# A transformer block with a mixture of experts: blocks of 32 slots on four column groups, longer runs of weights, and near buffers for half of the next expert

## The reference, cut to what matters

```python
logits = xt @ router_w + router_b                # 256 x 32
top_v, top_e = lax.top_k(logits, 4)
wts = softmax(top_v)
hgu = xb @ w_gate_up[e] + b_gate_up[e]           # 1024 -> 2048
gate, up = split(hgu, 2)
gate = minimum(gate, 7.0); up = clip(up, -7.0, 7.0)
act = (up + 1.0) * (gate * sigmoid(1.702 * gate))
y = act @ w_down[e] + b_down[e]                  # 1024 -> 1024
```

```text
2 127 71 46 36 3 24 88 50 22 16 23 33 11 17 99 61 5 28 28 7 3 9 30 27 16 15 37 2 20 16 52
```

## Time and profile before

| | us |
|---|---|
| median of 3 runs | 1495.45 |
| lowest, highest | 1490.48, 1495.61 |
| the profiled execution | 1494.09 |
| its span | 1492.1 |
| TensorE, VectorE, ScalarE, GpSimd busy | 1395.6, 450.2, 254.9, 10.6 |

### The profile page before, as it was taken

The page is one execution under the profiler, slowest core; times in us unless marked ns, Lnnn a source line. Parts: engine busy times, 40 slices in busy tenths (PEclk is TensorE's granted clock), DMA queues, the critical chain, the costliest instruction groups (busy, mean ns, idle before and its releaser), DMA issues.

```text
span 1492.1 us, 17242 instructions
## 1 busy us (share of the span) xinstructions
PE 1395.6 (94%) x6391; PEld 619.5 (42%) x6392; DVE 450.2 (30%) x965; ACT 254.9 (17%) x435; POOL 10.6 (1%) x34
## 2 busy tenths in 40 slices
PE   5999999999969999999999999999999999989996
PEld 3888455777533333333333333233333333223321
DVE  2240033131252332332333333233333332323233
ACT  3311024100021111111111111111111111111111
POOL 0000000100000000000000000000000000000000
PEclk9999999999978999999999999999999999999998
DMA  9734332788546367999699999979999999999994
GB/s 353 258 117 166 116 134 92 256 301 321 191 168 264 146 265 288 418 418 419 245 419 417 417 419 419 417 306 413 418 418 419 416 418 419 418 417 417 419 419 200
DMA packets 113087, 483.37 MB, mean 324 GB/s; under 512 B 10102, under 2 KB 10266, under 8 KB 80202
## 3 DMA queue, kind: packets, MB, share of 16 engines
q1 hardware_dynamic: 111666, 477.95, 80.2%
q0 software_dynamic: 1056, 4.06, 0.9%
q10 hardware_dynamic: 344, 1.07, 0.2%
HBM read 482.00 MB, written 1.05 MB: 324 GB/s over the span
## 4 chain that ended last, share of the span: by engine, by line
PE 72%; DMA 12%; SPq 9%; ACT 4%; issue 1%; DVE 1%; DVEq 0%; ACTq 0%
PE bank L1383 23%; PE bank L1074 14%; PE bank L1412 13%; DMA gu_slot<-in_w_gate_up 10%; PE bank L1083 7%; SPq L335 4%; SPq L340 4%; PE bank L1342 4%; PE bank L1358 3%; PE bank L1351 1%; DMA piece<-in_w_ada 1%; ACT gx L636 1%; ACT xg L638 1%; ACT actT L640 1%; PE bank L1062 1%
## 5 line engine op out<-in xcount | busy, mean ns | idle before, releaser
L1383 PE MATMUL bank<-gu_slot,xg 128*64 128x512 f32 x2304 | 518.4, 597 | 17.2 <-DMA gu_slot<-in_w_gate_up 16.5
L1383 PEld LDWEIGHTS bank<-gu_slot,xg 128*64 128x64 f32 x2304 | 159.5, 137 | 364.7 <-issue 307.5
L1412 PE MATMUL bank<-dn_slot,actT 128*64 128x512 f32 x1152 | 255.1, 595 | 24.7 <-ACT actT L640 24.7
L994 DVE TENSOR_TENSOR rowt<-bank,gt 128x512 f32<-128x512 f32 x144 | 92.8, 687 | 397.2 <-PE bank L1358 396.0
L1074 PE MATMUL bank<-hT,piece 128*128 128x256 f32 x704 | 155.5, 383 | 0.4 <-DMA piece<-in_w_in 0.4
L1412 PEld LDWEIGHTS bank<-dn_slot,actT 128*64 128x64 f32 x1152 | 79.5, 137 | 177.2 <-issue 143.9
L1074 PEld LDWEIGHTS bank<-hT,piece 128*128 128x128 f32 x704 | 134.3, 192 | 21.2 <-issue 2.0
L634 ACT ACTIVATE sig<-gcl 128x512 f32<-128x512 f32 x36 | 22.7, 630 | 569.2 <-DVE gcl L1012 569.2
L1012 DVE TENSOR_SCALAR gcl<-bank 128x512 f32<-128x512 f32 x36 | 24.9, 691 | 273.2 <-PE bank L1383 273.2
L998 DVE TENSOR_TENSOR xs<-xs,rowt 128x512 f32<-128x512 f32 x144 | 93.1, 688 | 2.5
L1083 PE MATMUL bank<-piece,hT 128*128 128x512 f32 x192 | 83.4, 593 | 0.0
(11 more groups left out here) (278 smaller groups left out, 772.6 us busy)
## 6 DMA issues: line engine op xcount, KB each, us to landing
gu_slot<-in_w_gate_up SPq DMA_DIRECT2D x256, 1024.0 KB, 17.2
dn_slot<-in_w_down SPq DMA_DIRECT2D x128, 1024.0 KB, 17.5
piece<-in_w_in SPq DMA_DIRECT2D x17, 2048.0 KB, 8.7
piece<-in_w_ada SPq DMA_DIRECT2D x12, 2048.0 KB, 15.0
piece<-in_w_branch_a SPq DMA_DIRECT2D x2, 2048.0 KB, 7.9
piece<-in_w_branch_b SPq DMA_DIRECT2D x2, 2048.0 KB, 8.6
piece<-in_w_out SPq DMA_DIRECT2D x2, 2048.0 KB, 10.5
xs<-in_x ACTq DMA_DIRECT2D x1, 1024.0 KB, 8.8
```

Of the source, the lines that this page charges most:

```text
L994: ins = V.tensor_tensor(rowt[:, t, :], sum_bank[t][q][:], gt2[:, cols_], ALU.mult)
L1383: ins = M(bank[u][64 * q:64 * q + 64, :], xg[:, k % 4, 64 * (k // 4):64 * (k // 4) + 64], gu_slot[k][:, cols_], start=(k == 0), stop=(k == ...
L1412: ins = M(bank[5][64 * q:64 * q + 64, :], actT[:, f % 4, 64 * (f // 4):64 * (f // 4) + 64], dn_slot[f // 2][:, f % 2, 512 * q:512 * q + 51 ...
```

## The change

- A block has 32 slots. Gate-up, bias, gather and down run on four column groups of 32: each group makes a quarter of the output columns (256 gate and 256 up in one product of 512, or 256 down columns). The scatter has four row groups of 32 into four PSUM banks, in two turns; the second waits for the first (`scatter_half`).
- The order of a block on TensorE is new: gate-up pieces 0 and 1, gather of the next block, down of the block before, gate-up piece 2, bias, piece 3, scatter and transposes, transposes of the hidden values.
- The sum over blocks stays in four PSUM banks; `add_rows` is gone. The expert bias rows start it, behind block 0 (`bias_done`). VectorE copies the transposed hidden values.
- Gate-up weights come in four pieces of 2 MiB with two neighbouring rows per partition, a run of 16 KB; down in four pieces of 1 MiB in runs of 8 KB.
- Pieces 0 and 1 of both, of expert e+1, are loaded into near buffers (`gu_land`, `dn_land`, 6 MiB), and GpSimd copies them into the slots when the last block of expert e has used these: eight copies of 128x1024 for gate-up and four for down, per expert. Pieces 2 and 3 are loaded straight into their slots, once they are used. Expert 1's near pieces are loaded ahead of the loop.
- Each expert has at least one block.

The core of the diff (in the TensorE part only new and kept lines):

```diff
 PAD = -2.0e38
-SLOTS = 64
+SLOTS = 32
...
         piece = [sb(f"piece{i}", 16 * i, [P, KT, 512]) for i in range(NP2)]
-        gu_slot = [sb(f"gu_slot{j}", 8 * j, [P, 2048]) for j in range(8)]
+        gu_slot = [sb(f"gu_slot{j}", 16 * j, [P, 2, 2, D]) for j in range(4)]
...
+        gu_land = [sb(f"gu_land{q}", 136 + 16 * q, [P, 2, 2, D]) for q in range(2)]
+        dn_land = [sb(f"dn_land{q}", 168 + 8 * q, [P, 2, D]) for q in range(2)]
...
-        sum_bank = [[bank[6], bank[7]], [bank[4], bank[5]]]
+        hid_bank, y_bank, turn_bank, xgT_bank = bank[4], bank[5], bank[6], bank[7]
+        sum_bank = [[bank[0], bank[1]], [bank[2], bank[3]]]
...
+            def gate_up_rows(e, q):
+                rows = slice(2 * P * q, 2 * P * (q + 1))
+                return (w_gate_up[0, e, rows, :].rearrange("(p r) n -> p (r n)", r=2) if isinstance(e, int) else
+                        w_gate_up[0, ds(e, 1), rows, :].rearrange("a (p r) n -> p (a r n)", r=2))
...
+            def load_gate_up(e, q):
+                sp.dma_start(gu_slot[q][:].rearrange("p r u n -> p (r u n)"), gate_up_rows(e, q)).then_inc(gu_in[q], 16)
...
-                user = [last for n, (_, _, last) in enumerate(PIECES) if n % NP2 == j // 2][-1]
+                    load_down(0, 2 * (kind == "wb") + i)
+            for q in range(4):
+                user = [last for n, (_, _, last) in enumerate(PIECES) if n % NP2 == q][-1]
                 wait_tile(sp, user)
-                load_expert_piece(0, j)
+                load_gate_up(0, q)
+            sp.wait_ge(bias3_ready, 1)
+            land_gate_up(1, 0)
+            wait_tile(sp, "rp")
...
+            sp.wait_ge(h2_ready, 4)
...
+            sp.wait_ge(bias_done, 1)
+            land_down(1, 1)
...
+            def second_half(e):
+                free = sp.value_load(table_used[0:1, e:e + 1] if isinstance(e, int) else table_used[0:1, ds(e, 1)],
+                                     min_val=1, max_val=MAXB + 1)
+                for q in (2, 3):
+                    sp.wait_ge(gu_in[q], 16 * e)
+                    sp.wait_ge(gu_used[q] if q < 3 else gu_full, free)
+                    load_gate_up(e, q)
+                for q in (2, 3):
+                    sp.wait_ge(dn_in[q], 16 * e)
+                    sp.wait_ge(dn_used[q] if q < 3 else y_full, free)
+                    load_down(e, q)
+            with sp.Fori(1, E - 1) as e:
+                second_half(e)
+                for q in range(2):
+                    sp.wait_ge(gu_in[q], 16 * e + 16)
+                    land_gate_up(sp.snap(e + 1), q)
+                for q in range(2):
+                    sp.wait_ge(dn_in[q], 16 * e + 16)
+                    land_down(sp.snap(e + 1), q)
+            second_half(E - 1)
...
+            pool.wait_ge(tables_ready, 1)
+            with pool.Fori(1, E) as e:
+                free = pool.value_load(table_used[0:1, ds(e, 1)], min_val=1, max_val=MAXB + 1)
+                for q in range(2):
+                    pool.wait_ge(gu_near[q], 16 * e)
+                    pool.wait_ge(gu_used[q], free)
+                    for r in range(2):
+                        for u in range(2):
+                            nc.gpsimd.tensor_copy(gu_slot[q][:, r, u, :], gu_land[q][:, r, u, :]).then_inc(gu_in[q], 4)
+                for q in range(2):
+                    pool.wait_ge(dn_near[q], 16 * e)
+                    pool.wait_ge(dn_used[q], free)
+                    for r in range(2):
+                        nc.gpsimd.tensor_copy(dn_slot[q][:, r, :], dn_land[q][:, r, :]).then_inc(dn_in[q], 8)
         @block.scalar
...
-                act.wait_ge(selwT_full, g1_)
-                A(selwT[:], bank[1][:, 0:T], ACT.Copy).then_inc(selw_out, 1)
-                act.wait_ge(y_full, g2_)
-                A(ysb[:], bank[5][:], ACT.Copy).then_inc(y_out, 1)
+                take_gathered(g2_)
+                take_rows_out(g1_)
+                gate_curve(g1_)
+                take_turned(g2_)
+                take_weights(g1_)
+            take_rows_out(act.snap(nb + 1))
             step(A(warm[:, 0:1], ident[:, 0:1], ACT.Sqrt))
...
+            def hidden(full_count, count):
+                dve.wait_ge(gu_full, full_count)
+                V.tensor_scalar(gcl[:], hid_bank[:, 0:256], LIMIT, None, ALU.min).then_inc(gcl_ready, 1)
+                V.tensor_scalar(hid_bank[:, 256:512], hid_bank[:, 256:512], LIMIT, -LIMIT, ALU.min, ALU.max)
+                dve.wait_ge(sig_ready, count)
+                V.scalar_tensor_tensor(gcl[:], hid_bank[:, 0:256], LIMIT, sig[:], ALU.min, ALU.mult).then_inc(gs_ready, 1)
+                dve.wait_ge(gs_ready, count)
+                V.scalar_tensor_tensor(act_t[:], hid_bank[:, 256:512], 1.0, gcl[:], ALU.add, ALU.mult).then_inc(act_ready, 1)
+                dve.wait_ge(actT_full, count)
+                V.tensor_copy(actT[:].rearrange("p r s -> p (r s)"), turn_bank[:, 0:256]).then_inc(actT_out, 1)
...
+                g2_ = dve.snap(g + 2)
+                e_next = dve.value_load(table_e[0:1, ds(g + 1, 1)], min_val=0, max_val=E - 1)
+                e_after = dve.value_load(table_e[0:1, ds(g + 2, 1)], min_val=0, max_val=E - 1)
+                hidden(g2_, g1_)
                 dve.wait_ge(selwT_full, g1_)
-                select_weights(e, ds(g + 1, 1))
-            dve.wait_ge(acc_out, dve.snap(nb + 1))
-            for t in range(TT):
-                dve.wait_ge(last_full, t + 1)
+                select_weights(e_next, ds(g + 1, 1))
+                dve.wait_ge(gath_full, g2_)
+                dve.wait_ge(selw_ready, g2_)
+                next_slots(g2_)
+                select(e_after)
...
+                for t in range(TT):
+                    for c in range(GROUPS):
+                        ins = M(turn_bank[32 * c:32 * c + 32, 0:256], sel[:, t, :], h2[:, t, 256 * c:256 * c + 256],
+                                start=(t == 0), stop=(t == TT - 1))
+                ins.then_inc(gath_full, 1)
+            def gather_transposes():
+                for r in range(2):
+                    ins = nc.tensor.transpose(xgT_bank[:, r * P:(r + 1) * P], gx[:].rearrange("p (i r) -> p r i", r=2)[:, r, :],
+                                              ident[:])
+                ins.then_inc(gxT_full, 1)
+            def weight_transposes():
+                for t in range(TT):
+                    ins = nc.tensor.transpose(y_bank[:, t * P:(t + 1) * P], selw[:, t, :, :].rearrange("p a s -> p (a s)"), ident[:])
+                ins.then_inc(selwT_full, 1)
+            def hidden_transposes():
+                for r in range(2):
+                    ins = nc.tensor.transpose(turn_bank[:, r * P:(r + 1) * P], act_t[:].rearrange("p (i r) -> p r i", r=2)[:, r, :],
+                                              ident[:])
+                ins.then_inc(actT_full, 1)
+            def gate_up(q, landed):
+                pe.wait_ge(gu_in[q], landed)
+                for r in range(2):
+                    for c in range(GROUPS):
+                        ins = M(hid_bank[32 * c:32 * c + 32, :], xg[:, r, 32 * q:32 * q + 32],
+                                gu_slot[q][:, r, :, 256 * c:256 * c + 256], start=(q == 0 and r == 0), stop=(q == 3 and r == 1))
+                ins.then_inc(gu_used[q] if q < 3 else gu_full, 1)
+            def gate_up_bias():
+                for c in range(GROUPS):
+                    M(hid_bank[32 * c:32 * c + 32, :], esel[:],
+                      bias3[:].rearrange("p (u n) -> p u n", u=2)[:, :, 256 * c:256 * c + 256], start=False, stop=False)
+            def down(landed):
+                for q in range(4):
+                    pe.wait_ge(dn_in[q], landed)
+                    for r in range(2):
+                        for c in range(GROUPS):
+                            ins = M(y_bank[32 * c:32 * c + 32, 0:256], actT[:, r, 32 * q:32 * q + 32],
+                                    dn_slot[q][:, r, 256 * c:256 * c + 256], start=(q == 0 and r == 0), stop=(q == 3 and r == 1))
+                    ins.then_inc(dn_used[q] if q < 3 else y_full, 1)
+            def scatter(turn, last=False):
+                for c in range(GROUPS):
+                    t = (c + turn) % 2
+                    ins = M(sum_bank[t][c // 2][:, 256 * (c % 2):256 * (c % 2) + 256], selwT[32 * c:32 * c + 32, t * P:(t + 1) * P],
+                            ysb[32 * c:32 * c + 32, :], start=False, stop=(last and turn == 1))
+                if last and turn == 1:
+                    ins.then_inc(last_full, 1)
+                if turn == 0:
+                    ins.then_inc(scatter_half, 1)
+            def bias_rows():
                 for t in range(TT):
                     for q in range(2):
+                        ins = M(sum_bank[t][q][:], wT[:, t * P:(t + 1) * P], bd[:, 512 * q:512 * q + 512], start=True, stop=False)
+                ins.then_inc(bias_done, 1)
             pe.wait_ge(bias3_ready, 1)
             pe.wait_ge(tables_ready, 1)
```

(44 more changed lines are left out.)

276 lines of the change are left out of this document (102 added, 174 removed).

## The result

| | us |
|---|---|
| median of 4 runs after | 1540.20 (1535.68 to 1545.03) |
| median of 4 runs before | 1495.43 (1490.48 to 1495.61) |
| ratio | 1.0307, 95% interval 1.0271 to 1.0343 |
| profiled execution, its span | 1535.68, 1534.0 |

A forecast was written before the change was run, and what follows sets the result against it. TensorE bound the early blocks, DMA the late experts at nearly equal price. From 475 us, 889 of loads and 77.6 of surpluses reach 1441; last blocks and end make 1486, with clock and median offset 1493; range 1470 to 1540.

The forecast's parts named there:

- Between the last gate-up and the next block lies a chain: TensorE's wait from a block's last gate-up through VectorE's and ScalarE's steps and two transposes: 3.0 us per block.
- 14.5 us. Bounds: 13.9 [...] 15.5: TensorE's time per block of 32 slots: gate-up 6.95, bias 0.22, gather 0.87, down 3.5 and chain 3.0.
- two more register loads cost 1: At the start, before block 0's gate-up: two added register loads cost 1 us, against 2.5 saved on gather and copies.
- the clock was held at full speed wherever blocks crowd: Experts with several blocks: TensorE at full clock, 14.5 us a block; half clock was expected only after rests in one-block experts.
- The pair of two-block experts 3 and 4 takes 29.0 a piece on TensorE and adds none: Two-block experts 3 and 4: TensorE's 29.0 us each stays under the 29.64 of loads, so no surplus.
- 77.6 forecast: Total surplus over 29.6 us an expert: expert 1 22.5, expert 2 14.2, expert 7 11.0, expert 15 25.5, plus restarts.
- the clock's 4 us: One-block experts: half clock after TensorE's rests makes the deciding copy path 0.2 us too long in some 22 experts.
- The rival of the longer block: A block takes 15.5 us, so crowded experts, two-block experts, start and tail take longer: 1510 us; chance 0.12.
- The copy path at half clock: Near-piece landing, copies, gate-up, gather, down, issue: 16.9 against 14.8 us in 22 experts; 1535, slowest copy about 1545; chance 0.25.
- the rival of useless wide runs: Loads: longer runs bring nothing, 29.9 us an expert, +7 us over 30 experts: 1500 us; chance 0.04.
- the landing buffers then carry the change alone: If the wide runs bring nothing, the near buffers alone make the gain, at 1500 us.
- TensorE waits for no piece: Expert 1: TensorE never waits for a load there, so its second-half interval is 52.1 us, a surplus of 22.5.

The follow-up runs named there:

- e1: Changed kernel with the edge of TensorE's loop moved behind the down product, its order of work unchanged: 1500.27 us, ratio 1.0035 to the kernel before.
- run 48: Not a follow-up run: the words say that the two register loads in the body of TensorE's loop run 48 times.
- e2: Changed kernel with two more unused register loads at the head of TensorE's loop in each block: 1595.07 us, ratio 1.0668 to the kernel before.
- e4: Changed kernel with the wide runs undone, 8 KB for gate-up and 4 KB for down, in the same four and four pieces: 1552.10 us.
- e8: Kernel before, 64 slots, with only the long runs added (16 KB gate-up, 8 KB down): 1490.14 us, ratio 0.9960 to the kernel before.
- e7: Changed kernel with the loop edge moved and without near buffers and GpSimd copies: 1494.36 us, ratio 1.0000 to the kernel before.
- e10: Changed kernel without near buffers and GpSimd copies, its TensorE loop left as the change has it: 1532.50 us, ratio 1.0263 to the kernel before.
- e9: Changed kernel with the loop edge moved, near buffers kept, and expert 1's second gate-up half issued ahead of the wait for bias rows: 1496.13 us.
- e5: Changed kernel with the loop edge moved and the next expert's near gate-up pieces issued ahead of the late down pieces: 1524.24 us, ratio 1.0195.

## Why the prediction was wrong

**The step that failed** is the block: "Between the last gate-up and the next block lies a chain", 3.0 us, and with it "14.5 us. Bounds: 13.9 [...] 15.5". Chain and matmuls came as forecast (14.58 in e1), but the term of the loop's edge is missing: 1.56 us at the place where the new order leaves TensorE nothing queued, 15.58 in all, beyond the upper bound. The register loads were seen, but as "two more register loads cost 1" at the start only; they stand in the loop's body and run 48 times. In the kernel before, the chain of the earlier trace rows has scatter, gate-up and gather back to back, and I read that as a loop that costs nothing, rather than as one whose edge lay under queued matmuls. I should have asked, for the changed order, what TensorE has queued at the edge.

**The second step** hangs on it: the clock was held at full speed wherever blocks crowd. The granted clock of 0.79 and 0.57 there, and 5.30 for 3.64, came with the rest: e1, with 0.4 of it left, shows 1.00, and e2, with 2.9, has more such blocks. e1 to e2 show both effects together; what each is worth by itself was not separated.

**"The pair of two-block experts 3 and 4 takes 29.0 a piece on TensorE and adds none"** stood 0.6 us from its limit, and part of the price comes from there: 5 us behind expert 12 and 4 behind expert 27, both of two blocks, for none forecast; the rest lies with the three and four blocks of the crowded experts and with the two-block experts right behind them. Between fourth gate-up pieces on which TensorE waits (at 480.78 for expert 1, then experts 6, 7, 11, 12, 15, 25, 27, 29), and last expert 31 at 1493.30, the time over 29.52 an expert sums to 127 us for 77.6 forecast, +49. With the clock's 4 us, which did not come, and 3.6 less for the loads, that is 42 of the 44 us between the span forecast (1490) and the 1534.0 of the profiled execution; the median lay 6 above this span where 3.4 was taken. The rival of the longer block had the size of the block, 15.5 us, from other causes (the scatter's wait and the narrow records, which came as forecast), and the wrong price: 17 us, with ten blocks and 31 us for a two-block expert, without the half clock. Its chance was 0.12.

**The copy path at half clock**, the rival with 1535 and a chance of 0.25, gives nearly the measured time and is wrong. In a one-block expert of after:

```profile
1327.39 4.00 POOL L480 COPY gu_slot<-gu_land 128x1024 f32<-128x1024 f32 x4 [0.90 <-issue]
```

From here, the landing of near piece 1, it is 11.4 us to the issue of the late down pieces at 1338.80, with the gate-up piece between them at half clock (3.60), and 9.7 where it ran at full clock (1297.87 to 1307.59), for 15.1 and 11.6 forecast, which had in them the time from the issue to the first byte as well; 14.8 would be the limit. DMA moves 427 GB/s from 1300 to 1400. So the clock's 4 us in the sum did not come in these experts. The Trainium skill (TensorE: Matmul & The Clock Gate, on the thin-M case) has every tile behind a wait start cold. In after that holds for gate-up piece 0 (3.64 us for 16 records at 1297.12 and 1326.63) and for piece 1 in one of these two experts (3.60, the other 1.92), not for gather and down (1.05 and 3.63 or 3.64 in both, as in the crowded blocks). A time that fits is no evidence for its mechanism. Nor does that rival's 1545 for the slowest copy come out of its own sum: four copies 0.4 us longer on a path that counts 22 times are 35 us on 1535.

**What held.** The loads: 29.52 for 29.64, that is 3.6 us better over 30 experts; e4 and e8 show from both sides that the run length does it, so the rival of useless wide runs falls. A copy takes 1.044 us for 1.1. The Trainium skill (GPSIMD Engine Reference, 3.1) has 1.03 cycles an element for simple bodies and 1.8 for the best tight loop at 1.2 GHz; 1.044 us for 1024 elements are 1.22 by that clock, nearer to the first. The start: third piece of expert 1 at 475.87 for 475. The tail: from expert 31's fourth piece (1493.30) to the span's end 40.7 us, with a transfer of 4.9 before it 45.6 from the third, for 45 forecast. Not so the near halves: "the landing buffers then carry the change alone" falls with e7 and e10. "TensorE waits for no piece" in expert 1 missed by 3.7 us (0.91 and 2.77), since its second half goes out only behind `bias_done`.

The parts of the change, then, each from a pair of runs: long runs −5 us in the kernel before (e8), −12 in the changed one (e4); near buffers, with the later issue at expert 1 that came with them, +8 (e10) or +6 (e7 against e1), of which e9 wins back 4; the edge and its clock +40 (e1), or +38 without near buffers (e10 against e7). Column groups of 32 slots with neither near buffers nor the bad edge (e7) are 4 us behind 64 slots with the same runs (e8): TensorE's lower load buys nothing. In most slices of the second half the loads set the time in both kernels, with 424 to 429 GB/s in e8's page and 422 to 428 in e7's; what the 4 us are was not looked into. The version to keep of all that ran is e8.

## What to carry to other kernels

When a change reorders a loop's body, look at where the loop's edge falls: register loads and the branch cost 0.4 us a turn here behind 64 queued matmuls and 1.56 behind a wait for another engine. When two limits lie within two per cent of each other, as 29.15 and 29.52 here, a small term decides which one holds and is then multiplied by every turn of the loop; give that margin a term of its own. A buffer that lets loads run ahead is worth what it takes off the rest of DMA from end to end, so ask also when the loads start again behind it.

## What the hardware showed beyond that

A register load from a table in on-chip memory is 0.30 us on TensorE's sequencer, and one added to the loop's edge lengthened the rest by 0.67 (e2). The Trainium skill (Advanced Engine Details and Errata, Control Flow Timing) has 108 ns for a compare-and-branch; here its records span 76 to 243 ns, median 208.

TensorE's granted clock fell within a stretch in which the engine was busy for 6.38 of 8 us (0.79, window 516 to 524), with rests of no more than 1.62 us since 490; in e1, with rests of 0.4 us at the edge, it stayed at 1.00 for the 110 us from 490.

In e5, where the copies begin right behind the transposes, VectorE's selection of weights stretches from 337 to 567 ns in the mean, and the copies of GpSimd run beside it. From e5's timeline:

```profile
1250.79 1.31 DVE L1058 TENSOR_SCALAR selw<-iota,slot_id,wts 128x128 f32<-128x128 f32 x2
1250.88 4.09 POOL L489 COPY gu_slot<-gu_land 128x1024 f32<-128x1024 f32 x4 [11.14 <-issue]
1252.23 0.82 DVE L1064 TENSOR_SCALAR iota<-iota 128x32 f32<-128x32 f32 x1
```

Without copies beside them the same two take 0.59 and 0.18. The Trainium skill (SBUF — State Buffer, "SBUF: two separate sides") says that GpSimd shares a pair of ports with VectorE, where VectorE runs in a mode of two ports or has two inputs in SBUF, and that one of them holds it for a whole instruction. The trace agrees in kind: the longest single selection, 1.114 us for 0.334, is 0.78 longer, less than one copy of 1.04. Whether this instruction runs in such a mode no run here shows. In after and e1 the copies fall elsewhere, and the mean is 337 and 336.
